# Four chunks instead of two multiplied quarter by quarter while the first modulation weights load

## What is computed

```python
mod = c_act @ mod_w[i] + mod_b[i]                     # 2048 x 12288 weights, one row
sh_m, sc_m, g_m, sh_f, sc_f, g_f = jnp.split(mod, 6, axis=-1)
h = modulate(rmsnorm(x, norm_mix_g[i]), sh_m, sc_m)   # h * (1 + scale) + shift
proj = h @ w_in                                       # gla_mixer
q, k, v, r, g1 = jnp.split(proj, [hk, 2*hk, 2*hk + hv, 2*hk + 2*hv], axis=-1)
log_a = jax.nn.log_sigmoid(g1 @ w_gate2 + b_gate) / 16
o = gla_chunked(q * DK ** -0.5, k, v, log_a)
o = rmsnorm(o, head_g) * jax.nn.silu(r)
y = o @ w_o
x = x + (1 + g_m) * y
```

## Time and profile before

| | us |
|---|---|
| median of 3 runs | 2342.28 |
| lowest, highest | 2336.43, 2348.26 |
| the profiled execution: its time | 2340.14 |
| its span in the trace | 2338.1 |
| mean granted TensorE clock | 0.99 of 2.4 GHz |
| PE busy | 2278.4 (97%) |
| DVE busy | 1791.0 (77%) |
| ACT busy | 1093.3 (47%) |

### The profile page before, as it was taken

How to read it: one execution, slowest core, us unless ns; L and a number is a source line. 1 busy time by engine, 2 the same in 40 slices (tenths; PEclk the granted TensorE clock), 3 DMA queues, 4 the chain that set the end, 5 groups by cost and what they waited for, 6 DMA issues and landing times. The chain is left out here.

```text
span 2338.1 us, 27127 instructions
## 1 busy us (share of the span) xinstructions
PE 2278.4 (97%) x10976; PEld 1865.2 (80%) x10976; DVE 1791.0 (77%) x1729; ACT 1093.3 (47%) x1193; POOL 34.0 (1%) x103
## 2 busy tenths in 40 slices
PE   5899999999999999999999999999999999999998
PEld 2578887788888888888888889888888888888886
DVE  2368987888998988889988779987786556565566
ACT  2244443445554344543555555444654445544454
POOL 0020000000000000000000000000000000000000
PEclk8999999999999999999999999999999999999999
DMA  9967789797987998889978377886775555555554
GB/s 363 387 206 286 261 300 361 266 335 274 353 318 292 347 348 311 298 318 374 335 269 307 126 248 258 306 321 236 261 296 204 193 196 181 180 197 191 187 184 158
DMA packets 259809, 632.93 MB, mean 271 GB/s; under 512 B 23505, under 2 KB 32745, under 8 KB 233978
## 3 DMA queue, kind: packets, MB, share of 16 engines
q1 hardware_dynamic: 258050, 625.90, 74.5%
q10 hardware_dynamic: 1656, 5.60, 0.6%
HBM read 629.36 MB, written 2.10 MB: 270 GB/s over the span
## 5 line engine op out<-in xcount | busy, mean ns | idle before, releaser
L1223 DVE TENSOR_TENSOR w_lo<-raw,w_hi 128x2048 fp32r<-128x2048 f32 (+1 forms) x378 | 840.2, 2224 | 337.5 <-ACT w_hi L758 335.5
L758 ACT ACTIVATE w_hi<-raw 128x2048 fp32r<-128x2048 f32 (+1 forms) x378 | 703.6, 1863 | 696.5 <-DMA raw<-in_ffn_w_up_dram 245.9
L1974 PE MATMUL gm<-w_hi,h_hi 128*128 128x512 f32 x1816 | 724.3, 399 | 6.8 <-DVE h_lo L1351 6.8
L1975 PE MATMUL gm<-w_hi,h_lo 128*128 128x512 f32 x1816 | 711.4, 392 | 0.0
L1981 PE MATMUL gm<-w_lo,h_hi 128*128 128x512 f32 x1816 | 448.8, 389 | 0.0
L1240 DVE SCALAR_TENSOR_TENSOR acc<-mods,c_col,acc 128x2048 f32<-128x2048 f32 x180 | 422.0, 2345 | 2.3 <-DMA mods<-in_mod_w_dram 1.6
L1974 PEld LDWEIGHTS gm<-w_hi,h_hi 128*128 128x128 f32 x1816 | 343.4, 189 | 84.0 <-DVE h_lo L1351 11.3
L1975 PEld LDWEIGHTS gm<-w_hi,h_lo 128*128 128x128 f32 x1816 | 343.5, 189 | 70.6 <-issue 1.7
L1981 PEld LDWEIGHTS gm<-w_lo,h_hi 128*128 128x128 f32 x1816 | 340.9, 188 | 70.8
L1974 PE MATMUL gm<-w_hi,a_hi 128*128 128x512 f32 x674 | 266.6, 396 | 0.8 <-ACT w_hi L758 0.8
L1975 PE MATMUL gm<-w_hi,a_lo 128*128 128x512 f32 x674 | 262.5, 390 | 0.0
(11 more groups left out here) (289 smaller groups left out, 2000.4 us busy)
## 6 DMA issues: line engine op xcount, KB each, us to landing
raw<-in_ffn_w_up_dram SPq DMA_DIRECT2D x176, 1024.0 KB, 4.9
mods<-in_mod_w_dram SPq DMA_DIRECT2D x170, 1024.0 KB, 7.1
raw<-in_ffn_w_down_dram SPq DMA_DIRECT2D x64, 1024.0 KB, 5.1
raw<-in_gla_w_in_dram SPq DMA_DIRECT2D x48, 1024.0 KB, 5.2
mods<-in_kv_mod_w_dram SPq DMA_DIRECT2D x32, 1024.0 KB, 6.8
raw<-in_ffn_w_down_dram SPq DMA_DIRECT2D x32, 768.0 KB, 4.6
raw<-in_gla_w_o_dram SPq DMA_DIRECT2D x16, 1024.0 KB, 7.2
raw<-in_mla_w_o_dram SPq DMA_DIRECT2D x16, 1024.0 KB, 6.9
```

Source lines behind the costliest of these rows:

```text
L758: act.activation(w_hi[:, k % RAW, 0:words], raw[:, k % RAW, 0:words], ACT.Copy).then_inc(hi_made, 1)
L1223: dve.tensor_tensor(w_lo[:, k % RAW, 0:words], raw[:, k % RAW, 0:words], w_hi[:, k % RAW, 0:words].bitcast(F32), ALU.subtract).then_inc(lo ...
L1974: pe.matmul(o, hi_s[:, kt, tok], wh[:, j, :], start=kt == 0, stop=False)
L1975: pe.matmul(o, lo_s[:, kt, tok], wh[:, j, :], start=False, stop=False)
```

## The change

Four chunks are multiplied in the loading phase instead of two: q0, q1 and the first two chunks of r (the output gate). The two PSUM buffers can't hold four running sums, so each item of this phase is a sum of its own (`alone=True`), and DVE takes it out (`add_part`): a copy to SBUF for quarter 0, an addition afterwards. The q chunks get all four quarters there (their last addition writes `u`, in the place of ACT's `evac`). The r chunks get quarters 0 to 2; their last item stands at the start of section r, which goes from 16 items to 10, and ACT's Silu of these two reads SBUF. The loading phase has 14 items instead of 8. The ring of preload tiles shrinks from 5 and 7 slots to 4 and 5. All modulation tiles that stood at the steps of the old r are laid out anew: k 11 instead of 7 (two each at steps 0 to 3), v 13 instead of 12, r 10 instead of 17, `gla_out` 14 instead of 12 (two each at steps 6 and 8). The heads' work in r comes every second step in place of every third. The number of matmuls stays, apart from the reductions' order; DVE has 14 more operations of 128 x 1024.

```diff
-PRE = 5
-PRE_LATE = 2
+PRE = 4
+PRE_LATE = 1
...
-        ("q", 1, 8, 2, 4, 0),
+        ("head", 1, 12, 12, 0, 0),
+        ("q", 1, 2, 2, 4, 0),
...
-        ("r", 1, 16, 4, 0, 0),
+        ("r", 1, 10, 4, 0, 0),
...
+        PRE_AHEAD = [8 * q + k for q in range(3) for k in (5, 7, 8, 12)] + [len(PRE_TILES)]
...
-            ("k", 2, 0, (0, 1, 2, 3, 5, 6, 7)), ("v", 2, 7, (0, 1, 2, 4, 5, 6, 8, 9, 10)), ("v", 3, 0, (12, 13, 14)),
-            ("r", 3, 3, every[:13]), ("r", 4, 0, (13, 13, 14, 15)),
-            ("gla_out", 4, 4, tuple(range(2, 14))),
+            ("k", 2, 0, (0, 0, 1, 1, 2, 2, 3, 3, 5, 6, 7)), ("v", 2, 11, (0, 1, 2, 4, 5)),
+            ("v", 3, 0, (6, 8, 9, 10, 12, 13, 14, 15)), ("r", 3, 8, every[:8]), ("r", 4, 0, (8, 9)),
+            ("gla_out", 4, 2, tuple(sorted((*range(2, 14), 6, 8)))),
...
+            def add_part(q, j):
+
+                c = 4 * q + j
+                dve.wait_ge(item_used, c + 1)
+                part = q_part[:, j] if j < 2 else r_part[:, j - 2]
+                if q == 0:
+                    dve.tensor_copy(part, gm[:, c % 2]).then_inc(u_made, 1)
+                    return
+                dve.wait_ge(u_made, c)
+                dst = part if q < 3 else u[:, j]
+                dve.tensor_tensor(dst, gm[:, c % 2], part, ALU.add).then_inc(u_made, 1)
...
+                if q:
+                    add_part(q - 1, 0)
+                    add_part(q - 1, 1)
+                    lo(4 * q - 1)
                 if q < 3:
-                    lo(2 * q)
-                    lo(2 * q + 1)
+                    lo(4 * q)
+                if q:
+                    add_part(q - 1, 2)
+                if q < 3:
+                    lo(4 * q + 1)
                 pre_rows(q)
...
-                    q_item(q - 1, 0)
-                for m in range(8 * q + 2, 8 * q + 5):
+                    head_item(q - 1, 0)
+                for m in range(8 * q + 2, 8 * q + 4):
                     pre_row(m)
+                if q:
+                    head_item(q - 1, 1)
                 pre_turn(q)
-                if 0 < q < 3:
-                    q_item(q - 1, 1)
-                for m in range(8 * q + 5, 8 * q + 8):
+                for m in range(8 * q + 4, 8 * q + 6):
+                    pre_row(m)
+                if q:
+                    head_item(q - 1, 2)
+                for m in range(8 * q + 6, 8 * q + 8):
                     pre_row(m)
                 pre_reduce(q)
-            q_item(2, 1)
-            for ch in range(2):
-                q_item(3, ch)
+                if q:
+                    head_item(q - 1, 3)
+            for j in range(2):
+                head_item(3, j)
```

More of the change, by code:

```diff
@@ L643, in _ @@
                         load_mod(*m)
-                if n < 8 and n % 2:
-                    for m in (4 * n + 2, 4 * n + 3):
-                        load_pre(m)
-                if n == 8:
+                if n == a["gate"].item:
                     sp.dma_start(wg2[0:RANK, :], gla_w_gate2[0]).then_inc(wg_in, 16)
@@ L905, in _ @@
                     act.activation(cos[:, :, :], ang[:, 1], ACT.Sin).then_inc(sin_made, 1)
-            hi(8)
-            hi(9)
-            evac(6, 0, u[:, 0])
-            hi(10)
-            evac(7, 1, u[:, 1])
-            hi(11)
+            for n in range(12, 18):
+                hi(n)
             def gate_size(f):
@@ L965, in _ @@
             s = a["r"]
-            for k in range(16):
-                if k < 15:
+            for k in range(10):
+                if k < 9:
                     hi(s.item + AHEAD + k)
@@ L1659, in _ @@
             s = a["r"]
-            for k in range(16):
+            for k in range(10):
                 score_step(16 + k)
-                if 3 <= k < 7:
-                    gate_row(2, k - 3)
-                if k in (8, 11, 14):
-                    gated_head((8, 11, 14).index(k))
-                if k < 15:
+                if k in (1, 2):
+                    ch = k - 1
+                    dve.wait_ge(item_used, s.item + ch + 1)
+                    dve.wait_ge(u_made, s.chunk + ch)
+                    dve.tensor_tensor(r_part[:, ch], gm[:, ch], r_part[:, ch], ALU.add).then_inc(u_made, 1)
+                if k in (2, 3):
+                    gate_row(2, k - 2)
+                if k == 4:
+                    gate_row(2, 2)
+                    gate_row(2, 3)
+                if k in (6, 8):
+                    gated_head((6, 8).index(k))
+                if k < 9:
                     mods_at(s.item + k)
@@ L1956, in item @@
             def item(n, slot, hi_s, lo_s, par, q, k_tiles=KT_ITEM, width=W, total=KT, turn=None,
-                     halves=False, middle=None):
+                     halves=False, middle=None, alone=False):
                 pe.wait_ge(lo_made if turn or halves else hi_made, n + 1)
@@ L1961, in item @@
                 wl = w_lo[:, slot % RAW, 0:k_tiles * width].rearrange("p (j n) -> p j n", j=k_tiles)
+                first, final = (q * k_tiles, q * k_tiles + k_tiles - 1) if alone else (0, total - 1)
                 def product(j, t):
@@ L1973, in high @@
                     o, tok = gm[:, par, t, 0:width], slice(t * P, (t + 1) * P)
-                    pe.matmul(o, hi_s[:, kt, tok], wh[:, j, :], start=kt == 0, stop=False)
+                    pe.matmul(o, hi_s[:, kt, tok], wh[:, j, :], start=kt == first, stop=False)
                     pe.matmul(o, lo_s[:, kt, tok], wh[:, j, :], start=False, stop=False)
@@ L2159, in pre_turn, with head_item @@
                     turn_fill("norm0", f, xn)
-            def q_item(q, ch):
+            def head_item(q, j):
                 pe.wait_ge(tp_free, a["norm0"].tp + 2 * q + 2)
-                item(2 * q + ch, 2 * q + ch, h_hi, h_lo, ch, q)
+                n = 4 * q + j
+                gm_free(n)
+                item(n, n, h_hi, h_lo, n % 2, q, alone=True)
             pe.wait_ge(consts, 1)
@@ L2313, in _ @@
             s = a["r"]
-            for k in range(16):
-                if k % 4 == 0:
-                    gm_free(s.chunk + k // 4)
-                item(s.item + k, s.item + k, h_hi, h_lo, (k // 4) % 2, k % 4)
+            for k in range(10):
+                ch, q = (k, 3) if k < 2 else (2 + (k - 2) // 4, (k - 2) % 4)
+                if k < 2 or q == 0:
+                    gm_free(s.chunk + ch)
+                item(s.item + k, s.item + k, h_hi, h_lo, ch % 2, q, alone=k < 2)
                 if k < 2:
                     scores(14 + k)
-                if 2 <= k < 6:
-                    reduce_mod(2, (k - 2,))
-                if k == 6:
+                if k in (1, 2):
+                    reduce_mod(2, (k - 1,))
+                if k == 3:
+                    reduce_mod(2, (2, 3))
+                if k == 4:
                     pe.wait_ge(u_made, a["v"].chunk + 4)
-                if k in (6, 9, 12):
-                    head_out((6, 9, 12).index(k))
-                if k == 13:
+                if k in (4, 6, 8):
+                    head_out((4, 6, 8).index(k))
+                if k == 9:
                     turn_head(0)
```

96 lines of the change are left out of this document (62 added, 34 removed).

## The result

The changed kernel takes 2353.3 us (median of five runs, 2351.8 to 2357.8). The kernel before, on the same chip beside it, takes 2342.3. The ratio is 1.0053, with a 95% interval of 1.0041 to 1.0065. So the change costs 8 to 12 us. The forecast was +4.3 us, 2346.6. The time lies inside the range given and at the far end of case A; the cost is two to three times the one forecast. The prediction took 0.5%, or 11.7 us, as the least that a measurement of this kernel can tell from no change; the intervals here reach only 0.12% to either side, about 3 us, so a cost of this size is measured and not noise.

The account below looks back on a forecast made before the run. PE was taken to bound the kernel (97% busy), except in the loading phase, which waits for data. Terms -5.8 (loading phase), +7.7 (section k) and +2.4 (gla_out) gave +4.3 on 2342.3: 2346.6 us, range 2332 to 2360.

Parts of the forecast that it names:

- case A: Whole kernel, the forecast itself: the loading phase wins a little, section k gives it back; 2338 to 2354 us, chance 0.52.
- loading phase: First item's end to gate: PE's idle or slow time falls from 17.1 to 11.3 us, so -5.8 us.
- section k: PE waits for the evacuation of the first k chunk: +7.7 us, from 5 to 10.
- v and r: Sections v and r: one more tile in v, one tile per item in r, no cost to PE: 0 us.
- gla_out, norm: End of gla_out: two more tiles, 4.7 us of DVE, delay the norm PE waits for: +2.4 us, between 1 and 4.1.
- Six items earlier, the waits: Loading phase: the wait for h goes; PE waits on DVE's copies before reductions, 3.4, 3.4 and 1.1, together 7.9 us.
- Half clock in the loading phase: Behind the loading phase's reductions: two stretches at half clock of 1.7 us each, 3.4 us; ends zero and three (5.1).
- Rival D, tiles late in the loading phase: Loading phase: PE waits for late tiles, two places in each of three quarters; +12 us on case A, 2359; chance 0.20.
- The gap in the transfers: Loading phase: the DMA queue is dry from some 52 to 61.7 us, which costs nothing by itself.
- Two tiles at each of k0 to k3: Section k: tiles ahead of items in SP's queue make item k6 and ACT's evacuation late; PE waits 7.7 us.
- Rival B: Section k: the wait is hidden, tiles land sooner or PE's need moves; 2339 us, no measurable change; chance 0.16.
- Rival C, no cost anywhere: Loading phase fills fully, no half clock or reduction waits, k's wait hidden: 2328 us, faster by over 0.5%; chance 0.12.

Follow-up runs that it names:

- after_again: The changed kernel itself, unedited, timed and profiled once more on another chip: 2351.7 us, ratio 1.0032 to the kernel before.
- spread2: Changed kernel with a second layout of the modulation tiles (two ahead of k, k 8, v 14, r 12, gla_out 12), loading phase untouched: 2339.5 us, ratio 0.999.
- spread: Changed kernel with a first other layout of the modulation tiles (two ahead of k, k 7, v 13, r 14, gla_out 12): ratio 1.0074.
- b_k11: Kernel before with only k's tiles changed: two at each of steps k0 to k3, fewer in v: 2352.3 us, ratio 1.0041.
- b_gla14: Kernel before with only 14 modulation tiles in gla_out instead of 12, two fewer at the end of r: ratio 1.0028, +6.6 us.
- k_evac_first: Changed kernel with ACT's evacuation of the first k chunk ahead of item k6's high half instead of behind it: 2352.4 us, ratio 1.0037.
- k_filler: Changed kernel with 66 extra products on PE, results overwritten, filling the wait ahead of the transposes out of u in k: ratio 1.004.
- spread2_lo: Changed kernel with the second tile layout and, in the loading phase, DVE's lo behind the reduction's copies: 2337.2 us, ratio 0.9975; again 2337.8, 0.9982.
- spread2_fill: spread2_lo with extra products on PE ahead of and within the last three reductions of the loading phase: 2341.6 us, ratio 0.9994.

## Why the prediction was right and wrong

The table has the terms as the two profiles of the changed kernel show them (changed, after_again), and as the timed runs show them. The loading phase goes by the gate's start, against 144.5 us, the mean of the three profiles with the phase of before, and less 32.6. Over all six profiles with the changed phase it starts at 175.7 on average, which is -1.4. For gla_out it is the distance from its first products behind `h_lo` to the norm's first transposes: 78.0 us before, 87.2 and 84.8 after.

| term | forecast | profiles | timed |
|---|---|---|---|
| loading phase | -5.8 | -5.0, +0.1; mean -1.4 | -4 and -9 (the sum less the two parts), about -5 (spread2) |
| section k | +7.7 | +11.2, +9.0 | alone +9.6 (6.6 to 12.7) |
| v and r | 0 | +0.3, -0.4 | |
| gla_out, norm | +2.4 | +9.2, +6.8 | alone +6.6 (4.4 to 8.7) |
| sum | +4.3 | +15.7, +15.5 | +8 to +12 |

The profiles' sum is above the timed one. The two profiled executions of the changed kernel are 4 us above its medians, and that of the kernel before is 2 below its own. The clock goes with that: the two have a mean clock of 0.984, all other runs of this kernel 0.985 to 0.990, and the eleven runs of spread2 go from 2335.8 us at 0.990 to 2344.9 at 0.986. A thousandth of the clock is 2.3 us. So the profiled executions are those with more half clock than usual, and the loading phase has to be judged by the timed column.

- *Six items earlier, the waits*: right. They end on DVE's copies, 2.1, 3.0 and 0.9 us for 3.4, 3.4 and 1.1; the 17.1 us of the phase before were counted rightly, no `h_lo` is waited for, and the added additions take 1.22 us (1.25).
- *Half clock in the loading phase*: the mechanism right, the size right or too small by which runs one asks. Two stretches of 1.7 us were taken, 3.4 in all, with three as the end. Six profiles with this phase lost 5.1 to 10.3 us at half clock between 58 us and the gate, against 5.2 in that of the kernel before. Less this loss, the gate starts at 166.9 to 167.2 in five of them (164.4 in spread, whose first 58 us had 3.4 us less of it) against 137.8 before (137.6 and 135.8 in b_k11 and b_gla14). That is 29.1 to 29.4 later, and 32.6 less the 4.0 that the forecast gave the waits without the clock (17.1 - 5.2 - 7.9) is 28.6. So the waits were right within 1 to 2 us, and what the profiles show beyond -5.8 is clock. In the timed runs, with less of it, the whole term comes out at -4 to -9 around the forecast. The Trainium skill ("TensorE: Matmul & The Clock Gate", section on HAM oscillation) has the clock fall at each long enough pause. The clock did fall behind all three reductions in four of the six profiles and behind two in the others. By that rule the term would have been -4.1; the runs do not decide between that and -5.8.
- *Rival D, tiles late in the loading phase*: wrong. One landing was waited for, 0.67 us. The gap in the transfers is there as forecast (94 GB/s between 56 and 60 us) and costs nothing.
- *Two tiles at each of k0 to k3*: right in its place, chain and size (8.17 and 7.22 for 7.7). b_k11 shows that the tiles alone do it, and k_evac_first that ACT's evacuation came last, with DVE's log decays close behind, held back by the same late item; the prediction had them inside the wait. The step that is missing is the clock behind the wait, 1.4 to 2.7 us (k_filler), though the same text priced half clock behind the reductions. Rival B is refuted.
- *v and r*: right.
- *gla_out*: the step that failed, +6.6 us in time for +2.4. "If nothing on DVE gives way the delay is 4.7 - 0.6 = 4.1" was set as the upper end. It counted DVE's work alone and did not ask what the second tile does in SP's queue, which was followed item by item in k. There the pair takes 8 to 9 us to go out, DVE then idles for the item behind it, and its last chunk comes 6 to 7 us late, not 4.7. The premise was wrong too, that "the norm behind it is what PE waits for": PE did not wait for the norm before, and now waits ahead of its last item, for that item's `lo` (3.15 and 3.48 us). It pays that, 1.35 us for the last modulation tile in one profile, and half clock on the reduction and first transposes. How much of the delay is the tiles' work on DVE and how much SP's queue was not measured apart.
- *Rival C, no cost anywhere*: wrong for this kernel. It gave 14 us; spread2_lo, with other places for the tiles, has 4 to 6 of them.

## What to carry to other kernels

When work moves out of a section, everything that was scheduled step by step beside it needs new places; here 48 tiles lost six steps, and their pairs cost more (16 us by the two parts) than the move won (about 5). With two slots and one in-order queue a pair of loads costs its turn-around (8 us here) to whatever stands behind it, so follow each pair's next item to the engine that needs it, in every section alike. And a wait of several microseconds on PE costs the wait plus the half clock behind it; filler keeps the clock up, but no run here shows that it wins time: in a pause that is there anyway it cost nothing (1.0040 beside 1.0053 and 1.0032), and around short pauses it cost 3 to 4 us.

## What was not expected of the hardware

- The granted clock after a pause differs between executions of one program: 0.86 or 0.57 in the same 12 us, and 5 us at the gate's start. One profile is not enough to size a half-clock term; set the profiled execution's time and mean clock beside those of the other runs first.
- Runs with a higher clock are not always faster: the runs of spread2_fill have a mean clock of 0.991 in the median and those of spread2_lo 0.990, and spread2_fill is the slower by 4 us.
